# A decoder layer's delta heads: three sums of squares as fp32r products with ones

## The chip, the cores and the metric

The kernel runs on one core of a Trainium2 chip. The metric is the device time of one execution, in microseconds (us). TensorE multiplies (its weight loads are listed as an engine of their own, PEld), VectorE (DVE), ScalarE (ACT) and GpSimd (POOL) work element by element, and SyncE (SP) issues most of the transfers. PSUM is the accumulator that TensorE writes; the kernel uses its eight banks of 128x512 float32 by hand.

## The reference

One hybrid decoder layer over 1024 tokens of width 1024: an RMSNorm, one projection that feeds dilated window attention (12 heads) and a gated DeltaNet (8 heads), sigmoid gates that merge the two, an output projection, and a SwiGLU MLP. What matters here is the DeltaNet branch:

```
qkv = silu(causal_depthwise_conv(concat([qd, kd, vd]), conv_w))
qd = l2norm(qd) * HEAD_DIM_K ** -0.5      # t * rsqrt(sum(t * t) + EPS) over the head's 128
kd = l2norm(kd)
o_d = gated_delta_rule(qd, kd, vd, g, beta)            # chunkwise
o_d = rmsnorm(o_d, dn_norm) * silu(z)                   # o_d * rsqrt(mean(o_d * o_d) + EPS)
```

So each head needs three sums of squares over its 128 channels, of q, of k and of its output, for each of 1024 tokens.

## The kernel before

All is laid out with channels on the 128 partitions and tokens along the free dimension, so a sum over a head's channels is a product with a 128x128 matrix of ones: it sums over partitions and leaves the sum on each of them.

The program is written by hand, engine by engine, with semaphores. `delta_iteration` is one iteration over a delta head. It has 64 steps j. In each step TensorE does one k of the dense projection (`dense_k`, L196: three fp32r products of 128x512, since weights and activations are split into a high and a low part), and beside it stand, in an order fixed by tables, the steps of the recurrence of the head before (`STEPS_AT`: in iteration h they belong to head h-1) and the preparation of head h: the convolution's taps (`TAPS_AT`, DVE), SiLU (`SILU_AT`, ACT), the squares of q and k (`SQUARE_AT`, at j = 47 and 49, ACT), the load of the decay rows (`ROWS_AT`, j = 60, DMAs issued by ACT) and their preparation on DVE (`PREPARE_AT`, j = 62). Every engine runs through its own list of this program in order. Iteration 0 is peeled and has the end of the attention beside it (`attention_end`, whose last mixing on DVE stands at j = 57 and 58, L757 to L764); heads 1 to 7 are a loop (`delta_heads`), and `delta_end` does the last head's recurrence beside the first gate projections, without taps.

The steps on which the change bears:

- `ss` (j = 4): TensorE multiplies ones by `sq[i]` for q and k (L1153, two halves each, float32). ACT takes a logarithm and an exponential of it (L1269, L1272), then DVE makes `qn` and `kn` (L1344, L1347). `kt0` (j = 15, L1167) is the first step of TensorE that waits for `kn`. The merge levels `y1` (L1198) and on follow.
- `a0` to `a7` and `b0` to `b7` (j = 45 to 60): the recurrence over eight chunks of 128 tokens. In `a`, TensorE multiplies by the state (L1247, L1248) and DVE forms `u_now` (L1398). In `b`, TensorE waits for `u_now`, multiplies by it (L1252, L1253), and DVE updates `state` (L1402), for which the next `a` waits.
- in `b3` and `b7`, when four chunks are done, ACT copies half of the output out of PSUM and squares it (L1325, L1326; in the trace `beta_v` and `beta_k`, whose space `o_raw` and `o_sq` share).
- `os` (j = 62): TensorE multiplies ones by `o_sq`, in halves (L1258, float32). `on`, at the end of the iteration, takes logarithm and exponential (ACT, L1330, L1333) and scales the output (DVE, L1406, L1409). Before it ACT reads the dense product `z_next` (L1430, j = 63).

`load_rows` (L1534) issues its three DMAs behind ACT's step b7, and DVE's preparation waits for them at L1458.

Of the kernel before, what the change touches and what calls it, by code (L numbers as in the profile page):

```python
# [65 lines left out]
def build(nc, x, norm_mix, w_in, conv_w, a_log, dt_bias, dn_norm, w_proj_attn, w_proj_delta,  # L66
          w_out, norm_ffn, w_gate, w_up, w_down, norm_final, out):
    ctx = ExitStack()
    with ctx:
# [31 lines left out]
        ident = keep("ident", [P, P])  # L101
        ones = keep("ones", [P, P])
        band = keep("band", [P, 2, 256])
        band_pair = keep("band_pair", [P, P])
# [171 lines left out]
        def setup_pool(pool, then):  # L276
# [23 lines left out]
            for h in range(NHA):  # L300
                g.memset(slopes[:, h:h + 1], float(2.0 ** (-8.0 * (h + 1) / NHA)) * DILATION[h // NSLOT])
            pool.drain().then_inc(consts, 1)

# [763 lines left out]
        def dt_(name, shape):  # L1067
# [25 lines left out]
        a_right, inv_right = dt_("a_right", [P, HALF]), dt_("inv_right", [P, HALF])  # L1093
        assert d0[0] <= work + 81920, d0[0] - work
        u_bar, w_t = inv, half_way
        o_raw, o_sq = beta_v, beta_k

        dl = {x_: sem("dl_" + x_) for x_ in (
            "read", "conv", "silu", "sq", "ss", "ln", "normed", "vt", "bv", "kt", "kdec", "kk", "qk", "rows",
            "diff", "dec", "a", "pt", "t0t", "t0", "t0c", "y", "yc", "ar", "ir", "pr", "prc", "dt", "dtm", "tt", "ttc", "ub", "ubc", "wt", "wtc",  # L1100
            "qdec", "ws", "u", "o", "s", "sup", "z", "os", "osq", "oss", "oln", "oexp", "out", "stored", "zero", "col", "eye")}

# [33 lines left out]
        SILU_AT = {30: 0, 46: 1, 59: 2}  # L1136
        SQUARE_AT = {47: 0, 49: 1}
        ROWS_AT, PREPARE_AT = 60, 62

# [4 lines left out]
        def delta_pe(pe, h, step):  # L1144
            mm, tr = nc.tensor.matmul, nc.tensor.transpose
            two = h * 2
            if step == "ss":
                wait(pe, dl["sup"], h * NCH)
                wait(pe, dl["osq"], two)
                for i in range(2):  # L1150
                    pe.wait_ge(dl["sq"], two + (i + 1))
                    for half in range(2):
                        last = mm(bank[(X0, Y0)[i] + half][:, :], ones[:, :], sq[i][:, half * HALF:(half + 1) * HALF],  # L1153
                                  start=True, stop=True)
                    last.then_inc(dl["ss"], 1)
# [93 lines left out]
            elif step[0] == "b":  # L1249
                c = int(step[1])  # L1250
                pe.wait_ge(dl["u"], h * NCH + (c + 1))
                mm(bank[X1][:, 0:P], chunk(k_dec, c), u_now[:, :], start=True, stop=True).then_inc(dl["s"], 1)  # L1252
                mm(bank[Y0 + c // 4][:, (c % 4) * P:(c % 4 + 1) * P], u_now[:, :], chunk(decay, c),  # L1253
                   start=False, stop=True).then_inc(dl["o"], 1)
            elif step == "os":
                for half in range(2):
                    pe.wait_ge(dl["osq"], two + (half + 1))
                    mm(bank[Z0 + half][:, :], ones[:, :], o_sq[:, half * HALF:(half + 1) * HALF],  # L1258
                       start=True, stop=True).then_inc(dl["oss"], 1)

        def delta_act(act, h, step):
# [59 lines left out]
            elif step in ("b3", "b7"):  # L1321
# [3 lines left out]
                f(o_raw[:, half * HALF:(half + 1) * HALF], bank[Y0 + half][:, :], ACT.Copy)  # L1325
                f(o_sq[:, half * HALF:(half + 1) * HALF], bank[Y0 + half][:, :], ACT.Square).then_inc(dl["osq"], 1)  # L1326
            elif step == "on":
# [7 lines left out]
        def delta_vec(dve, h, step):  # L1335
# [63 lines left out]
            elif step[0] == "b":  # L1399
                c = int(step[1])  # L1400
                dve.wait_ge(dl["s"], h * NCH + (c + 1))
                v.scalar_tensor_tensor(state[:, :], state[:, :], decay_all[:, c:c + 1], bank[X1][:, 0:P],  # L1402
                                       ALU.mult, ALU.add).then_inc(dl["sup"], 1)
            elif step == "on":
                dve.wait_ge(dl["oexp"], h + 1)
                v.scalar_tensor_tensor(o_raw[:, :], o_raw[:, :], dn_norm_c[:, 0:1], o_sq[:, :], ALU.mult, ALU.mult)  # L1406
                dve.drain()
                dve.wait_ge(dl["z"], h + 1)
                v.tensor_tensor(z_now[:, :], o_raw[:, :], z_now[:, :], ALU.mult).then_inc(dl["out"], 1)  # L1409
# [36 lines left out]
        def square_delta_act(act, h, i):  # L1446

            act.wait_ge(dl["silu"], h * 3 + (i + 1))
            wait(act, dl["normed"], h * 2)
            nc.scalar.activation(sq[i][:, :], qkv[i][:, :], ACT.Square).then_inc(dl["sq"], 1)  # L1450

# [41 lines left out]
        def delta_iteration(eng, h, dense, own, side, mix=None):  # L1493

            conv, silu, square, rows_, prepare = own
            for j in range(64):
# [11 lines left out]
                if j in SQUARE_AT:  # L1508
                    square(eng, h, SQUARE_AT[j])
                if j == ROWS_AT:  # L1510
                    rows_(eng, h)
# [24 lines left out]

        OWN_ACT = (nothing, silu_delta_act, square_delta_act, load_rows, nothing)
        OWN_VEC = (conv_vec, nothing, nothing, nothing, prepare_vec)

# [656 lines left out]
        def _(pe):  # L2196
            setup_pe(pe)
            attention(pe, dense_att_pe, att_pe, nothing, decay_pe)
            delta_iteration(pe, 0, dense_delta_pe, [nothing] * 5, att_pe, nothing)

# [3 lines left out]
            pe.wait_ge(o_taken, 6 * NSLOT)  # L2204
            delta_heads(pe, dense_delta_pe, [nothing] * 5, delta_pe)
            delta_end(pe, gate_step_pe, delta_pe)
# [65 lines left out]
```

## Time and profile before

| | |
|---|---|
| three runs | 2349.39 us median, 2349.14 to 2349.42 |
| the profiled execution | 2351.21 us |
| its span in the trace | 2349.5 us |
| mean granted clock of TensorE | 0.987 |
| busy: TensorE (PE), weight loads, DVE, ACT, POOL | 97%, 80%, 41%, 35%, 21% |
| share of the ending chain on TensorE | 91% |
| delta heads' recurrences in the trace | 599.6 to about 1264 us |

A row of a timeline has the start from the span's start and the duration in us, the engine, the line of kernel.py, the operation, output<-inputs with their shapes, and the count of instructions that were merged into the row. In square brackets stands how long the engine was idle before it, and what released it. Durations of matmuls on TensorE overlap, so their pace is read from the starts. A granted clock of 1.00 is 2.4 GHz and 0.50 is 1.2 GHz.

### The profile page before, as it was taken

To read this page: it belongs to the slowest core of one execution; us is meant where nothing else is said; L and a number is where in the kernel's file an instruction comes from. 1 tells how busy PE (TensorE), PEld (TensorE's weight loads), DVE (VectorE), ACT (ScalarE), POOL (GpSimd) and SP (SyncE) were. 2 spreads that over 40 slices of the span, in tenths; PEclk is the share of its full clock that TensorE was granted. 3 is DMA by queue.
4 is the path that set the end of the run, shared out by engine and by line. 5 is a ranking of instruction groups with operands and counts; after the bars stand their busy time and mean duration, and the time that the engine had idled before them with its cause. 6 is when DMAs were issued, how large, how long until landed. Compare 5 with 4: busy or idle time off the path is not lost.

```text
span 2349.5 us, 31341 instructions
## 1 busy us (share of the span) xinstructions
PE 2268.2 (97%) x11304; PEld 1882.0 (80%) x11304; DVE 953.2 (41%) x1360; ACT 811.0 (35%) x1398; POOL 501.2 (21%) x359
## 2 busy tenths in 40 slices
PE   5999999999999999999999999997799999999997
PEld 4788888888788788888878888886688888888886
DVE  3512122122755564565542113332755555550143
ACT  4322323233554555555452220022433333330012
POOL 6253222212211111111112233331000000043330
PEclk8999999999999999999999999999899999999998
DMA  5112121202220221121033443341122222261211
GB/s 119 47 37 64 52 66 45 72 27 44 86 61 17 71 62 36 45 62 62 18 90 101 141 138 117 102 117 45 33 91 83 88 81 80 80 221 47 90 54 72
DMA packets 245975, 174.26 MB, mean 74 GB/s; under 512 B 41160, under 2 KB 223624, under 8 KB 245920
## 3 DMA queue, kind: packets, MB, share of 16 engines
q1 hardware_dynamic: 215856, 129.12, 18.9%
q10 hardware_dynamic: 30064, 44.39, 5.9%
q8 instruction: 36, 0.59, 0.1%
q14 instruction: 19, 0.16, 0.0%
HBM read 142.83 MB, written 30.65 MB: 74 GB/s over the span
## 4 chain that ended last, share of the span: by engine, by line
PE 91%; DVE 4%; ACT 2%; DVEq 1%; issue 1%; POOL 1%; DMA 1%; ACTq 1%; SPq 0%; POOLq 0%
PE bank L196 39%; PE bank L1802 17%; PE bank L2030 10%; PE bank L982 6%; PE bank L1215 2%; PE bank L1198 2%; PE bank L605 1%; PE bank L1153 1%; PE bank L1205 1%; PE bank L616 1%; PE bank L1252 1%; PE bank L1247 1%; PE bank L1248 1%; PE bank L1253 1%; PE bank L1234 1%
## 5 line engine op out<-in xcount | busy, mean ns | idle before, releaser
L196 PE MATMUL bank<-u_hi,w_hi 128*128 128x512 f32 x1472 | 631.0, 429 | 3.0 <-POOL w_lo L184 1.0
L196 PE MATMUL bank<-u_hi,w_lo 128*128 128x512 f32 x1472 | 577.5, 392 | 0.0
L196 PE MATMUL bank<-u_lo,w_hi 128*128 128x512 f32 x1472 | 575.5, 391 | 0.0
L182 POOL CAST w_hi<-raw 128x1024 fp32r<-128x1024 f32 (+1 forms) x108 | 109.5, 1014 | 1152.9 <-PE bank L196 923.9
L196 PEld LDWEIGHTS bank<-u_hi,w_lo 128*128 128x128 f32 x1472 | 276.5, 188 | 60.8
L196 PEld LDWEIGHTS bank<-u_hi,w_hi 128*128 128x128 f32 x1472 | 278.4, 189 | 48.5 <-issue 5.6
L196 PEld LDWEIGHTS bank<-u_lo,w_hi 128*128 128x128 f32 x1472 | 278.9, 189 | 42.3 <-issue 3.8
L184 POOL TENSOR_TENSOR w_lo<-raw,w_hi 128x1024 fp32r<-128x1024 f32 (+1 forms) x108 | 262.3, 2429 | 15.9 <-issue 0.7
L1990 POOL CAST dn_hi<-dn_raw 128x896 fp32r<-128x896 f32 (+1 forms) x24 | 25.4, 1060 | 590.0 <-DMA dn_raw<-in_w_down 481.7
L2030 PE MATMUL bank<-v_lo,dn_hi 128*128 128x512 f32 x352 | 136.9, 389 | 0.0
L2030 PE MATMUL bank<-v_hi,dn_hi 128*128 128x512 f32 x352 | 136.9, 389 | 0.0
L2030 PE MATMUL bank<-v_hi,dn_lo 128*128 128x512 f32 x352 | 136.9, 389 | 0.0
L1489 DVE SCALAR_TENSOR_TENSOR conv_out<-conv_in,conv_c,conv_out 128x1024 f32<-128x1024 f32 (+1 forms) x96 | 100.5, 1047 | 14.9 <-issue 12.0
L1802 PE MATMUL bank<-t_hi_t,p_hi_s 128*128 128x512 f32 x264 | 103.0, 390 | 2.5 <-ACT gate_out L1825 2.5
L1802 PE MATMUL bank<-t_lo_t,p_hi_s 128*128 128x512 f32 x264 | 102.7, 389 | 0.0
L1802 PE MATMUL bank<-t_hi_t,p_lo_s 128*128 128x512 f32 x264 | 102.7, 389 | 0.0
L1378 DVE COPY_PREDICATED inv<-merge_mask,bank 128x256 f32<-128x256 uint8 x96 | 45.5, 491 | 108.6 <-PE bank L1215 108.2
L663 ACT ACTIVATE prob<-score,neg_max 128x256 f32<-128x256 f32 (+1 forms) x96 | 44.6, 465 | 98.9 <-DVE neg_max L725 93.4
L2030 PEld LDWEIGHTS bank<-v_hi,dn_lo 128*128 128x128 f32 x352 | 66.1, 188 | 13.8
L2030 PEld LDWEIGHTS bank<-v_lo,dn_hi 128*128 128x128 f32 x352 | 66.1, 188 | 13.8
L1829 ACT ACTIVATE gate_out<-gate_out 128x512 f32<-128x512 f32 x44 | 27.8, 632 | 142.5 <-DVE gate_out L1845 142.5
L2030 PEld LDWEIGHTS bank<-v_hi,dn_hi 128*128 128x128 f32 x352 | 66.1, 188 | 13.6
(302 smaller groups left out, 3889.1 us busy)
## 6 DMA issues: line engine op xcount, KB each, us to landing
raw<-in_w_in SPq DMA_DIRECT2D x84, 512.0 KB, 3.8
row<-scr_rows ACTq DMA_DIRECT2D x24, 512.0 KB, 4.8
raw_gate<-in_w_gate SPq DMA_DIRECT2D x22, 512.0 KB, 3.8
raw_up<-in_w_up SPq DMA_DIRECT2D x22, 512.0 KB, 3.9
scr_v<-gate_out SPq DMA_DIRECT2D x44, 256.0 KB, 2.5
v_in<-scr_v SPq DMA_DIRECT2D x11, 1024.0 KB, 8.1
scr_gate<-tmp ACTq DMA_DIRECT2D x16, 512.0 KB, 2.9
tmp<-scr_gate ACTq DMA_DIRECT2D x16, 512.0 KB, 4.2
```

Source lines behind the costliest of these rows:

```text
L182: nc.gpsimd.tensor_copy(hi[:, 0:kt, :], raw[slot][:, 0:kt, :])
L184: nc.gpsimd.tensor_tensor(lo[:, 0:kt, :], raw[slot][:, 0:kt, :], hi[:, 0:kt, :].bitcast(F32), ALU.subtract).then_inc(weights_split, 1)
L196: last = nc.tensor.matmul(bank[dst][:, :], wpart[slot][wp][:, k, :], rhs[ap][:, k, half * HALF:(half + 1) * HALF], start=k == 0 and (wp, a ...
L663: last = nc.scalar.activation(prob[p % 2][:, i * w:(i + 1) * w], score[p % 2][:, i * w:(i + 1) * w], ACT.Exp, bias=neg_max[:, b:b + 1], ac ...
L982: last = nc.tensor.matmul(bank[dst][:, :], wpart[slot][wp][:, k, :], branch[ap][:, b, half * HALF:(half + 1) * HALF], start=start and (wp, ...
L1198: last = mm(by_block(chunk(bank[Y0], q), level), chunk(a_right, q), side_columns(inv[:, 2 * q * P:2 * (q + 1) * P], level, 0), start=True, ...
L1215: last = mm(bank[Z0 + half][:, (q % 2) * P:(q % 2 + 1) * P], chunk(inv_t, q), half_pair[:, q, :], start=True, stop=True)
L1378: v.copy_predicated(left(c4(inv, half), level), left(merge_mask[:, level:level + 1, :].broadcast_to([P, 4, P]), level), bank[Z0 + half][:, ...
L1489: last = v.scalar_tensor_tensor(conv_out[:, part], shifted, tap, conv_out[:, part], ALU.mult, ALU.add)
L1802: last = nc.tensor.matmul(dst[:, :], (p_hi, p_lo)[wp][name][:, kk, :], (t_hi, t_lo)[ap][o][:, kk, :], start=i in (0, 1, 3) and kk == 0 and ...
L1829: f(t[:, :], t[:, :], ACT.Silu).then_inc(up["silu"], 1)
L2030: last = nc.tensor.matmul(bank[DN_BANKS[g % 2][i][half]][:, :], dn_part[(n + i) % 4][wp][:, k, :], (v_hi, v_lo)[ap][(k0 + k) // 2][:, (k0 ...
```

## The change

The three products with float32 ones become products of fp32r ones with a high and a low part of the squares, both added up in the same bank. The high part is a cast of the square to fp32r, the low part is square minus high part.

For q and k, ACT squares as before at j = 47 and 49, then drains and casts to `sq_hi`; DVE subtracts at the new steps j = 58 and 60 (`square_low_vec`) and signals `sqlow`, for which TensorE waits in `ss`. `sq_hi` lies where `qn` and `kn` are, so ACT waits for steps that read them (`qdec`, `wt`) instead of `normed`. For the output, ACT drains and casts behind the square in b3 and b7, and signals `osq` only then; DVE waits for `osq` at the end of its own steps b3 and b7, subtracts and signals `osqlow`; TensorE takes high and low part in `os`. A copy of `ones` to `ones_r` is made on POOL in the setup.

```diff
+            g.tensor_copy(ones_r[:, :], ones[:, :])
...
+        sq_hi = [at(f"sq_hi{i}", [P, S], F32R, t) for i, t in enumerate((work + 20480, work + 32768))]
+        o_hi = at("o_hi", [P, S], F32R, work + 53248)
+        o_lo = at("o_lo", [P, S], F32R, work + 65536)
+        sq_lo = [at(f"sq_lo{i}", [P, S], F32R, work + 24576 + 4096 * i) for i in range(2)]
...
         SQUARE_AT = {47: 0, 49: 1}
+        SQUARE_LOW_AT = {58: 0, 60: 1}
...
                 for i in range(2):
-                    pe.wait_ge(dl["sq"], two + (i + 1))
+                    pe.wait_ge(dl["sqlow"], two + (i + 1))
                     for half in range(2):
-                        last = mm(bank[(X0, Y0)[i] + half][:, :], ones[:, :], sq[i][:, half * HALF:(half + 1) * HALF],
-                                  start=True, stop=True)
+                        for part in (sq_hi, sq_lo):
+                            last = mm(bank[(X0, Y0)[i] + half][:, :], ones_r[:, :],
+                                      part[i][:, half * HALF:(half + 1) * HALF],
+                                      start=part is sq_hi, stop=part is sq_lo)
                     last.then_inc(dl["ss"], 1)
...
             elif step == "os":
                 for half in range(2):
+                    hs = slice(half * HALF, (half + 1) * HALF)
                     pe.wait_ge(dl["osq"], two + (half + 1))
-                    mm(bank[Z0 + half][:, :], ones[:, :], o_sq[:, half * HALF:(half + 1) * HALF],
-                       start=True, stop=True).then_inc(dl["oss"], 1)
+                    mm(bank[Z0 + half][:, :], ones_r[:, :], o_hi[:, hs], start=True, stop=False)
+                    pe.wait_ge(dl["osqlow"], two + (half + 1))
+                    mm(bank[Z0 + half][:, :], ones_r[:, :], o_lo[:, hs], start=False, stop=True).then_inc(dl["oss"], 1)
...
-                f(o_sq[:, half * HALF:(half + 1) * HALF], bank[Y0 + half][:, :], ACT.Square).then_inc(dl["osq"], 1)
+                f(o_sq[:, half * HALF:(half + 1) * HALF], bank[Y0 + half][:, :], ACT.Square)
+                act.drain()
+                f(o_hi[:, half * HALF:(half + 1) * HALF], o_sq[:, half * HALF:(half + 1) * HALF],
+                  ACT.Copy).then_inc(dl["osq"], 1)
...
                 v.scalar_tensor_tensor(state[:, :], state[:, :], decay_all[:, c:c + 1], bank[X1][:, 0:P],
                                        ALU.mult, ALU.add).then_inc(dl["sup"], 1)
+                if c % 4 == 3:
+                    hs = slice((c // 4) * HALF, (c // 4 + 1) * HALF)
+                    dve.wait_ge(dl["osq"], two + (c // 4 + 1))
+                    v.tensor_tensor(o_lo[:, hs], o_sq[:, hs], o_hi[:, hs].bitcast(F32), ALU.subtract).then_inc(dl["osqlow"], 1)
...
             act.wait_ge(dl["silu"], h * 3 + (i + 1))
-            wait(act, dl["normed"], h * 2)
-            nc.scalar.activation(sq[i][:, :], qkv[i][:, :], ACT.Square).then_inc(dl["sq"], 1)
+            wait(act, dl["qdec"], h)
+            wait(act, dl["wt"], h * 2)
+            nc.scalar.activation(sq[i][:, :], qkv[i][:, :], ACT.Square)
+            act.drain()
+            nc.scalar.activation(sq_hi[i][:, :], sq[i][:, :], ACT.Copy).then_inc(dl["sq"], 1)
+
+        def square_low_vec(dve, h, i):
+
+            dve.wait_ge(dl["sq"], h * 2 + (i + 1))
+            nc.vector.tensor_tensor(sq_lo[i][:, :], sq[i][:, :], sq_hi[i][:, :].bitcast(F32),
+                                    ALU.subtract).then_inc(dl["sqlow"], 1)
...
                 if j in SQUARE_AT:
                     square(eng, h, SQUARE_AT[j])
+                if j in SQUARE_LOW_AT:
+                    square_low(eng, h, SQUARE_LOW_AT[j])
```

## Rows read from the trace of the kernel before

**Rows 1.** The page: busy time and share of TensorE; chain that ended last, by engine.

```profile
PE 2268.2 (97%) x11304; PEld 1882.0 (80%) x11304; DVE 953.2 (41%) x1360; ACT 811.0 (35%) x1398; POOL 501.2 (21%) x359
...
PE 91%; DVE 4%; ACT 2%; DVEq 1%; issue 1%; POOL 1%; DMA 1%; ACTq 1%; SPq 0%; POOLq 0%
```

**Rows 2.** Groups by line: shapes, xcount | busy us, mean ns | idle before.

```profile
L1153 PE MATMUL bank<-sq,ones 128*128 128x512 f32 x64 | 28.8, 592 | 0.0
...
L1258 PE MATMUL bank<-beta_k,ones 128*128 128x512 f32 x32 | 15.0, 592 | 0.0
```

**Rows 3.** Timeline, step ss of head 0: start us, us, engine, instruction.

```profile
599.85 3.60 PE L1153 MATMUL bank<-sq,ones 128*128 128x512 f32 x8
...
603.52 0.39 PE L196 MATMUL bank<-u_lo,w_hi 128*128 128x512 f32 x1
```

**Rows 4.** Chain that ended last, output projection: start us, us of 24 dense matmuls.

```profile
1559.79 5.46 PE bank L196 x24
```

**Rows 5.** Timeline, end of b7 and step os of head 0.

```profile
680.21 0.59 ACT L1326 ACTIVATE beta_k<-bank 128x512 f32<-128x512 f32 x1
...
680.90 1.88 PE L1258 MATMUL bank<-beta_k,ones 128*128 128x512 f32 x4
```

**Rows 6.** Timeline, steps b3 to b4 of head 0.

```profile
670.38 0.35 DVE L1402 SCALAR_TENSOR_TENSOR state<-state,decay_all,bank 128x128 f32<-128x128 f32 x1
...
670.60 0.60 ACT L1325 ACTIVATE beta_v<-bank 128x512 f32<-128x512 f32 x1 [2.77 <-PE bank L1253]
...
670.83 0.75 DVE L1489 SCALAR_TENSOR_TENSOR conv_out<-conv_in,conv_c,conv_out 128x512 f32<-128x512 f32 x1
...
671.09 0.59 ACT L1326 ACTIVATE beta_k<-bank 128x512 f32<-128x512 f32 x1
...
671.51 0.29 DVE L1398 TENSOR_TENSOR u_now<-inv,bank 128x128 f32<-128x128 f32 x1
...
672.23 0.38 PE L1252 MATMUL bank<-u_now,k_dec 128*128 128x128 f32 x2
```

**Rows 7.** Groups by line of other stages: casts on ACT, a subtraction on DVE.

```profile
L1714 ACT ACTIVATE p_hi_s<-p_sum_s 128x512 fp32r<-128x512 f32 x88 | 52.7, 622 | 8.2 <-DVE p_sum_s L1724 6.1
...
L948 ACT ACTIVATE b_hi<-tmp 128x1024 f32 x12 | 12.6, 1054 | 0.9 <-DMA tmp<-scr_branch 0.9
...
L1729 DVE TENSOR_TENSOR p_lo_s<-p_sum_s,p_hi_s 128x512 fp32r<-128x512 f32 x88 | 56.5, 684 | 0.0
```

**Rows 8.** Timeline of DVE, the preparation behind head 1's row DMAs.

```profile
687.39 0.17 DVE L1458 COPY decay_all<-row 128x8 f32<-128x8 f32 x1 [7.44 <-DMA row<-scr_rows]
```

**Rows 9.** Timeline of head 1, from the normalisation of q and k to kt0.

```profile
694.75 1.23 DVE L1344 SCALAR_TENSOR_TENSOR qn<-qkv,sq 128x1024 f32<-128x1024 f32 x1 [0.80 <-ACT sq L1272]
...
695.89 1.22 DVE L1347 TENSOR_TENSOR kn<-qkv,sq 128x1024 f32<-128x1024 f32 x1
...
698.59 0.60 PE L1167 MATMUL bank<-ident,kn 128*128 128x128 f32 x4
```

**Rows 10.** Timeline around head 0's sums, beside the end of the attention.

```profile
603.74 1.23 DVE L764 TENSOR_TENSOR joint<-joint,o_t 128x1024 f32<-128x1024 f32 x1
...
606.05 0.50 PE L196 MATMUL bank<-u_hi,w_hi 128*128 128x512 f32 x1 [0.55 <-ACT z_next L1430]
...
615.07 0.66 PE L1167 MATMUL bank<-ident,kn 128*128 128x128 f32 x4 [2.38 <-DVE kn L1347]
```

**Rows 11.** Timeline, step y1 of head 0 and of head 1.

```profile
625.67 1.07 PE L1198 MATMUL bank<-inv,a_right 128*128 128x128 f32 x8
...
708.79 1.07 PE L1198 MATMUL bank<-inv,a_right 128*128 128x128 f32 x8
```

**Rows 12.** Timeline; then stretches: us, busy by engine (x), granted clock, DMA share, GB/s.

```profile
47.29 0.79 PE L406 MATMUL bank<-u_hi,w_ba_hi 128*128 128x512 f32 x1 [3.68 <-POOL u_lo L307]
...
47.20:50.00 2.80, 2.71 (x6) 2.15 (x7) 0.00 (x0) 0.00 (x0) 2.65 (x3) 0.52 0.00 0
...
615.00:618.00 3.00, 2.93 (x21) 2.72 (x22) 3.00 (x2) 2.65 (x7) 2.26 (x1) 1.00 0.00 0
```

More of the change, by code:

```diff
@@ L102, in build @@
         ones = keep("ones", [P, P])
+        ones_r = keep("ones_r", [P, P], F32R)
         band = keep("band", [P, 2, 256])
@@ L1098, in build @@
         dl = {x_: sem("dl_" + x_) for x_ in (
-            "read", "conv", "silu", "sq", "ss", "ln", "normed", "vt", "bv", "kt", "kdec", "kk", "qk", "rows",
+            "read", "conv", "silu", "sq", "sqlow", "ss", "ln", "normed", "vt", "bv", "kt", "kdec", "kk", "qk", "rows",
             "diff", "dec", "a", "pt", "t0t", "t0", "t0c", "y", "yc", "ar", "ir", "pr", "prc", "dt", "dtm", "tt", "ttc", "ub", "ubc", "wt", "wtc",
-            "qdec", "ws", "u", "o", "s", "sup", "z", "os", "osq", "oss", "oln", "oexp", "out", "stored", "zero", "col", "eye")}
+            "qdec", "ws", "u", "o", "s", "sup", "z", "os", "osq", "osqlow", "oss", "oln", "oexp", "out", "stored", "zero", "col", "eye")}
         def side_columns(t, level, side):
@@ L1493, in delta_iteration @@
         def delta_iteration(eng, h, dense, own, side, mix=None):
-            conv, silu, square, rows_, prepare = own
+            conv, silu, square, square_low, rows_, prepare = own
             for j in range(64):
@@ L1534, in load_rows @@
                 act.dma_start(row[j][:, :], src.rearrange("a t -> (a t)").partition_broadcast(P)).then_inc(dl["rows"], 16)
-        OWN_ACT = (nothing, silu_delta_act, square_delta_act, load_rows, nothing)
-        OWN_VEC = (conv_vec, nothing, nothing, nothing, prepare_vec)
+        OWN_ACT = (nothing, silu_delta_act, square_delta_act, nothing, load_rows, nothing)
+        OWN_VEC = (conv_vec, nothing, nothing, square_low_vec, nothing, prepare_vec)
         def store_delta(sp, h):
@@ L2198, in _ @@
             attention(pe, dense_att_pe, att_pe, nothing, decay_pe)
-            delta_iteration(pe, 0, dense_delta_pe, [nothing] * 5, att_pe, nothing)
+            delta_iteration(pe, 0, dense_delta_pe, [nothing] * 6, att_pe, nothing)
             pe.wait_ge(st_copied, 3 * NSLOT)
@@ L2204, in _ @@
             pe.wait_ge(o_taken, 6 * NSLOT)
-            delta_heads(pe, dense_delta_pe, [nothing] * 5, delta_pe)
+            delta_heads(pe, dense_delta_pe, [nothing] * 6, delta_pe)
             delta_end(pe, gate_step_pe, delta_pe)
```

## The prediction

> **What bounds the kernel now.** I read the page first: TensorE is busy for 97% of the span and the chain that ended last lies 91% on it [rows 1]. A saving counts only where TensorE keeps its pace, and every wait put into its way costs in full. Then the groups by line: the ones products stand in the trace as 64 and 32 records, two to one 128x512 product, so 32 products for q and k and 16 for the output [rows 2]. Last the timelines of one head, with one question: when does each input of a changed step arrive, and when does TensorE come for it? The figures below are of head 0, whose steps begin at 599.85 us, and from its end at 680.9 us on of head 1; the next heads repeat them to a few hundredths of a us, save where I say so.
>
> **The products.** From the first ones record of q and k to the second dense matmul behind them pass 603.52 - 599.85 = 3.67 us [rows 3]. A dense fp32r matmul takes 5.46 / 24 = 0.227 us [rows 4], so the four float32 products take 3.67 - 0.23 = 3.44 us, 0.86 us each. After the change they are eight fp32r ones, 8 x 0.227 = 1.82 us: 1.62 us less in a head. The two of the output, from 680.90 on [rows 5], take 1.72 us by the same measure and become four, 0.91 us: 0.81 us less. With every input in time that is 8 x 2.43 = 19.4 us. Now the inputs.
>
> **q and k, heads 1 to 7: 1.3 us gained each.** Squares, casts and low parts are ready before TensorE comes: ACT has 2.77 us free ahead of its b3 step [rows 6] and gets two casts there (1054 ns for 128x1024 [rows 7]), 2.1 us; the two low parts (like kn's 1.22 us for the same shape [rows 9]) lie on DVE at j=58 and 60, where its taps are over, and ahead of its 7.44 us wait for the row DMA [rows 8]. Behind the sums ACT's two logarithms and exponentials go on from z_next at j=63 and do not move; kn is ready at 695.89 + 1.22 = 697.11, TensorE comes for it at 698.59 [rows 9]. It will come at 696.97, so it waits 0.2 us, plus 0.1 us for a weight load that is no longer hidden (a dense matmul right behind a wait lasts 0.50 us [rows 10], one in the stream 0.39 [rows 3]). Net 1.62 - 0.3 = 1.3 us; seven heads, -9.2 us. With no wait it is -11.3, with the row DMAs 1 us later reaching kn (DVE has 0.80 us of slack ahead of qn [rows 9]) some -8.
>
> **The output's step os: nothing gained.** The second half is squared by ACT until 680.21 + 0.59 = 680.80 [rows 5]. Behind it stand a drain and a cast (622 ns for 128x512, [rows 7]), to 681.5, then DVE's subtraction (684 ns, [rows 7]), to 682.2. The last product starts at 682.25, loads its weights in the open, and ends near 682.6, where the float32 version ends today (680.90 + 1.72 = 682.6). 0 us; the bounds over eight heads are -6.5 (all hidden) and +4 (each of the two operations slower by a quarter of a us).
>
> **Step b3, the new wait: 2.1 us lost per head.** At c = 3 DVE now waits for osq and subtracts before it goes on. DVE works its list in order, so behind the wait stand the conv tap of j=52 and u_now of chunk 4, for which TensorE's step b4 waits. ACT's square ends at 671.09 + 0.59 = 671.68 [rows 6]; drain and cast to 672.35; low part to 673.1; the tap starts 0.1 us later (as today behind state, 670.73 to 670.83) at 673.2, and u_now 0.68 us after the tap's start (671.51 - 670.83), at 673.9 instead of 671.51: 2.4 us late [rows 6]. u_now ends today at 671.80 and b4 starts at 672.23, which leaves 0.4 us of slack. TensorE loses 2.0 us, and 0.1 us for the open weight load: 2.1 us. Afterwards DVE needs about 2.1 us a chunk (two taps of 0.68, a state of 0.35, a u_now of 0.29, and the gaps between them), and TensorE takes twice 671.51 - 670.38, 2.26 us; so DVE catches up in two chunks without a further stall. Seven heads, +14.7 us; bounds 1.8 and 2.5 each (+12.6, +17.5). The last head has the same timing but no taps, so u_now would start at 673.05 in place of 671.51: 1.5 us late, less 0.4, plus 0.1: +1.2 us.
>
> The Trainium skill, "TensorE: Matmul & The Clock Gate", section "Architectural detail", says that ScalarE and VectorE take their queues strictly in order, and only TensorE pulls weight loads ahead. By that rule this wait is paid in full; were it not so, the sum would be without its largest term, about 16 us lower.
>
> **The normalisation of head 0: 3.2 us lost.** Here DVE has no idle time in front: the mixing of the attention output runs until 603.74 + 1.23 = 604.97 [rows 10], and the low part of q comes behind it in DVE's list, that of k behind that. They are ready at 606.1 and 607.3, but TensorE comes for them at 599.85 [rows 3]. It stands for 6.3 us, finishes both sums at 608.3, and after nine dense matmuls is at 610.4 where today it is at 606.05 [rows 10]: 4.3 us behind. Today it then waits until 615.07 for kn (2.38 us [rows 10]); it will come at 616.7 with kn ready at about 615. From there I take the flow of head 1, 10.2 us from kt0 at 698.59 to the first merge level at 708.79, which brings that level to 626.9 instead of 625.67 [rows 9, 11]: 1.3 us lost. On top comes the clock. After a gap of 3.68 us the granted clock was 0.52 over the next 2.8 us, after the 2.38 us gap at kn it was 1.00 [rows 12]. So after 6.3 us TensorE starts at 1.2 GHz; eight matmuls at 0.43 instead of 0.23 us cost 1.6 to 1.9 us, which nothing hides, since it is late already. Together +3.2 us, bounds +0.5 and +5.
>
> The same page, section "What's actually happening", says that an idle array falls back to half rate and is released again by sustained work; by it the 1.9 us are due, without it the first head costs 1.3 us.
>
> **Small parts, taken as nothing.** The copy into ones_r is one 128x128 operation on POOL in the setup, where POOL then waits for the first activations. The waits for qdec and wt at j=47 ask for steps of j=19 and 43. The row DMAs are issued about 1 us later, behind drain and cast; DVE waits for them anyway [rows 8], and what follows has that 0.8 us of slack [rows 9]. With this cover gone it would be 0.2 us a head.
>
> **Sum.** -9.2 + 0 + 14.7 + 1.2 + 3.2 = +9.9 us. The profiled execution took 2351.21 us with a span of 2349.5; the median of the runs is 2349.39, so I add the difference to the median, **2359.3 us**, or 2361.1 for a profiled execution.
>
> **The rivals.**
> 1. The wait at b3 does not reach TensorE (u_now is not held up, or osq arrives early enough). For it: each part is off TensorE, and DVE has time left in this stage. Against: the times of rows 6, which put ACT's square alone past u_now. The rest stays: -9.2 + 3.2 = -6.0, **2343.4 us**, faster. It decides for this side as soon as the stall at b3 falls below about 0.3 us a head; with the first head free too it is 2340. Chance 0.08.
> 2. The stalls exist but are smaller: b3 at 1.7 us (the tap runs closer behind), no slow clock and no loss in the first head: -9.2 + 11.9 + 1 = +3.7, **2353 us**, no change. Chance 0.14.
> 3. DVE does not catch up: the chunks behind b4 lose another 0.3 us, and os 0.5 us, in each of eight heads: +6.4 on the sum, **2365.7 us**. For it: DVE's load of 2.1 in 2.28 us leaves little. Against: state is due 0.4 us after DVE can have it. Chance 0.18.
> 4. The forecast, 0.60.
> That an fp32r product with ones is no faster is excluded by rows 2 to 4, shape for shape.
>
> **Numbers.** Slower by over 0.2% (4.7 us, about what a measurement of this kernel tells from no change) are the forecast, rival 3 and a little of rival 2: 0.80. Within: 0.12. Faster: 0.08. The range reaches from within rival 2 to rival 3's centre, 2352 to 2366, and leaves out rival 1 and the upper tail.
>
> **What the profile after will show.** The group of L1153 becomes two forms of fp32r, 0.227 us apart, 64 products, the output's 32. At b4 TensorE and its weight load stand idle for about 2 us on DVE's u_now in seven heads and 1.1 us in the last. At kt0 it waits about 0.2 us on kn. In the first head it stands for some 6 us before the first sum, followed by a granted clock near 0.5, and no longer waits at kn. The period of a head grows by about 0.8 us. The prediction is wrong if u_now of chunk 4 starts less than 1 us later than today relative to b3, or if the period falls.

## The result, and the profile of the changed kernel

The changed kernel takes 2370.35 us (2368.80 to 2372.88), the kernel before 2349.40 us (2349.14 to 2353.06) beside it: the ratio is 1.0086, 95% interval 1.0073 to 1.0099. It is slower, as forecast, but by 20.9 us where 9.9 were forecast, and above the range of 2352 to 2366. The profiled execution took 2370.46 us with a span of 2368.7. One of the four executions of the output-only kernel below took 2878.87 us at a mean granted clock of 0.749, a slower state of the chip, and is left out of its numbers.

Start with the places that the prediction named. The timeline of b3 and b4 in head 0 of the changed kernel (start us, us, engine, instruction) shows the chain that it worked out, link by link:

```profile
671.20 0.60 ACT L1336 ACTIVATE beta_v<-bank 128x512 f32<-128x512 f32 x1 [0.51 <-PE bank L1262]
...
671.70 0.59 ACT L1337 ACTIVATE beta_k<-bank 128x512 f32<-128x512 f32 x1
...
672.36 0.63 ACT L1339 ACTIVATE o_hi<-beta_k 128x512 fp32r<-128x512 f32 x1
...
673.02 0.69 DVE L1421 TENSOR_TENSOR o_lo<-beta_k,o_hi 128x512 fp32r<-128x512 f32 x1 [1.69 <-ACT o_hi L1339]
673.82 0.75 DVE L1516 SCALAR_TENSOR_TENSOR conv_out<-conv_in,conv_c,conv_out 128x512 f32<-128x512 f32 x1
674.48 0.28 DVE L1412 TENSOR_TENSOR u_now<-inv,bank 128x128 f32<-128x128 f32 x1
...
674.82 0.49 PE L1261 MATMUL bank<-u_now,k_dec 128*128 128x128 f32 x2 [1.81 <-DVE u_now L1412]
```

From ACT's copy at the end of b3 to u_now of chunk 4 pass 674.48 - 671.20 = 3.28 us, where they were 671.51 - 670.60 = 0.91 us [rows 6]: 2.37 us late, 2.4 forecast. The waits of TensorE over the seven loop heads and the last one (engine, line waited for: us in total, times, longest):

```profile
PE bank L1261 <- DVE u_now L1412: 13.7, 8, 1.8
PE bank L1270 <- DVE o_lo L1421: 1.9, 8, 0.2
PE bank L1224 <- issue: 1.3, 7, 0.2
PE bank L1176 <- DVE kn L1361: 1.0, 3, 0.5
```

In the kernel before, the same list held only the third line. A wait list tells what an engine stood for, not how fast it ran afterwards. That is in the granted clock. The stretches right behind the stall in head 0 (us, TensorE's busy time (x), granted clock, DMA share, GB/s):

```profile
673.20:674.80 1.60, 0.00 (x0) 1.00 0.00 0
674.90:676.10 1.20, 1.20 (x8) 1.00 0.00 0
676.10:679.60 3.50, 3.50 (x14) 0.54 0.01 2
679.60:684.00 4.40, 4.40 (x28) 0.98 0.00 0
```

TensorE resumes at 674.82 at 2.4 GHz, and some 1.6 us later, inside the third of these stretches, its clock falls to 1.2 GHz for 3.4 us. The matmuls show it too, a dense one lasting 0.63 us instead of 0.39:

```profile
675.60 0.39 PE L197 MATMUL bank<-u_lo,w_hi 128*128 128x512 f32 x1
...
677.17 0.63 PE L197 MATMUL bank<-u_lo,w_hi 128*128 128x512 f32 x1
```

This happens in all seven loop heads, and not in the last head, whose stall is 0.96 us. Four stretches of 10 us, from 2 us behind the copy of b3, in heads 0, 2, 6 and the last:

```profile
673.20:683.20 10.00, 8.38 (x42) 0.83 0.00 1
844.52:854.52 10.00, 8.38 (x42) 0.83 0.00 0
1186.39:1196.39 10.00, 8.38 (x42) 0.83 0.00 0
1272.49:1282.49 10.00, 9.24 (x54) 1.00 0.00 0
```

This is the reading by which the experiments below are judged: 0.83 means that the clock fell in that head, 1.00 that it did not.

**Where the 19.2 us of span went.** ACT's copy at the end of b3 and the one at the end of b7 cut each head in two. The sums of the pieces in the two profiled executions:

| stretch | before | after | difference | forecast |
|---|---|---|---|---|
| b3 to b7, seven loop heads | 7 x 9.12 | 7 x 12.8 | +25.9 | +14.7 |
| b3 to b7, last head | 9.12 | 10.35 | +1.2 | +1.2 |
| b7 to the next b3, seven times | 517.3 | 509.6 | -7.7 | -9.2 |
| span's start to the first b3 | 670.6 | 671.2 | +0.6 | +3.2 |
| last b7 to the end | 1088.7 | 1087.9 | -0.8 | 0 |

One line is off by more than 3 us, and it is the one with the slow clock in it.

### The profile page after: what moved, and what is told of

Its sections match the earlier page's. It is cut to its first block, busy times and chain, and to the rows that moved or that the text cites. A ratio compares the mean times of both kernels' runs of the same rounds, so it can differ in the third digit from the quotient of the medians.

```text
span 2368.7 us, 31452 instructions
## 1 busy us (share of the span) xinstructions
PE 2267.4 (96%) x11304; PEld 1887.4 (80%) x11304; DVE 985.9 (42%) x1392; ACT 838.2 (35%) x1430; POOL 504.2 (21%) x360
## 4 chain that ended last, share of the span: by engine, by line
PE 87%; DVE 4%; ACT 2%; DMA 2%; DVEq 1%; issue 1%; ACTq 1%; POOL 1%; SPq 0%; POOLq 0%
PE bank L197 37%; PE bank L1831 17%; PE bank L2059 10%; PE bank L984 6%; PE bank L1224 2%; PE bank L1207 2%; DMA row<-scr_rows 1%; PE bank L607 1%; PE bank L1214 1%; PE bank L1261 1%; PE bank L618 1%; PE bank L1262 1%; PE bank L1243 1%; PE bank L1181 1%; PE bank L1237 1%
## 5 line engine op out<-in xcount | busy, mean ns | idle before, releaser
L185 POOL TENSOR_TENSOR w_lo<-raw,w_hi 128x1024 fp32r<-128x1024 f32 (+1 forms) x108 | 263.9, 2444 | 15.6 <-issue 0.2
L1516 DVE SCALAR_TENSOR_TENSOR conv_out<-conv_in,conv_c,conv_out 128x1024 f32<-128x1024 f32 (+1 forms) x96 | 100.6, 1048 | 16.0 <-issue 13.7
L2059 PEld LDWEIGHTS bank<-v_hi,dn_hi 128*128 128x128 f32 x352 | 66.1, 188 | 14.2 <-POOL dn_lo L2021 0.4
```

The costliest lines, as they stand in the source:

```text
L185: nc.gpsimd.tensor_tensor(lo[:, 0:kt, :], raw[slot][:, 0:kt, :], hi[:, 0:kt, :].bitcast(F32), ALU.subtract).then_inc(weights_split, 1)
L1516: last = v.scalar_tensor_tensor(conv_out[:, part], shifted, tap, conv_out[:, part], ALU.mult, ALU.add)
L2059: last = nc.tensor.matmul(bank[DN_BANKS[g % 2][i][half]][:, :], dn_part[(n + i) % 4][wp][:, k, :], (v_hi, v_lo)[ap][(k0 + k) // 2][:, (k0 ...
```

## The experiments

**Theory.** The stall at b4 is as forecast, and it brings the clock down behind it; that second cost is what was missed. **Rival.** The missing 11 us have another cause (the new products, VectorE's backlog, a clock that falls in this stage anyway), and the slow clock is no consequence of the stall.

All kernels were timed beside the kernel before, which gave 2350.55 to 2351.06 us in these sessions. The full table first; "b3 to b7" in us, "slow heads" are loop heads in which the clock fell, both read from one profiled execution of each kernel:

| kernel | median us | wait at b4 | b3 to b7 | slow heads |
|---|---|---|---|---|
| before | 2350.9 | none | 9.12 | 0 of 7 |
| changed | 2370.35 | 1.81 | 12.8 | 7 of 7 |
| changed, again | 2370.25 | 1.81 | 11.34 / 12.8 | 6 of 7 |
| q and k only | 2344.72 | none | 9.12 | 0 of 7 |
| output only | 2367.70 | 1.81 | 11.27 / 12.8 | 2 of 7 |
| low part at chunk 6 | 2346.97 | none | 9.12 | 0 of 7 |
| filled, 8 products | 2363.67 | about 0.1 | 11.35 | 0 of 7 |
| filled, 4 products | 2363.06 | 0.9 | 11.34 | 0 of 7 |
| shifted by 0.45 us | 2370.00 | 1.81 | 11.34 / 12.8 | 4 of 7 |
| shifted by 1.36 us | 2370.13 | 1.81 | 11.34 / 12.8 | 2 of 7 |
| longer stall | 2388.71 | 3.42 | 12.88 / 14.2 to 15.6 | 6 of 7 |
| os at j=63 | 2343.52 | none | 9.12 | 0 of 7 |
| and head 0 early | 2342.93 | none | 9.12 | 0 of 7 |
| and kn first | 2344.23 | none | 9.12 | 0 of 7 |

The setup, ahead of this stage, varies from execution to execution (the first b3 lay between 669.4 and 674.3 us), so medians of two kernels closer than some 2 us are not told apart, and the intervals inside the traces are what the verdicts rest on.

**1. The q and k part alone.** The output goes back to one float32 product per half, and with it ACT's second cast and VectorE's wait go.

```
-                if c % 4 == 3:
-                    hs = slice((c // 4) * HALF, (c // 4 + 1) * HALF)
-                    dve.wait_ge(dl["osq"], two + (c // 4 + 1))
-                    v.tensor_tensor(o_lo[:, hs], o_sq[:, hs], o_hi[:, hs].bitcast(F32), ALU.subtract).then_inc(dl["osqlow"], 1)
...
+                    mm(bank[Z0 + half][:, :], ones[:, :], o_sq[:, half * HALF:(half + 1) * HALF],
+                       start=True, stop=True).then_inc(dl["oss"], 1)
```

> Only the q and k part of the change; the output's sum of squares stays the float32 product of the kernel before. My theory (the 2.0 us stall at b4 and the slow clock that follows it are the whole of what the prediction missed): no wait at b4, b3 to b7 back to 9.1 us, the granted clock after it 1.00 in all heads; what is left is -1.2 to -1.3 us in each of seven heads and +3.0 in head 0's normalisation, so 2349.4 - 8.7 + 3.0 = 2343.7 us. The rival (the missing 11 us have another cause, in the q and k part or in the clock of the stage as a whole): 2350 to 2355 us, with a lower clock somewhere in heads 1 to 7 although nothing stalls.

Measured: 2344.72 us (2342.83 to 2345.69), ratio 0.9971 (0.9960 to 0.9982), 6.1 us below the kernel before. b3 to b7 is 9.12 us in all heads. b7 to the next b3 is 72.6 us instead of 73.94 in six of the seven intervals, which is the 1.3 us per head of the prediction; the seventh, beside the first gate projection, is 73.30 instead of 73.56, since TensorE stands there for ACT to take that projection out of its bank (`tmp`). No wait on u_now, o_lo or kn is left among TensorE's:

```profile
PE bank L1224 <- issue: 1.3, 7, 0.2
PE bank L197 <- ACT tmp L916: 0.9, 1, 0.9
```

So the cast and low-part work for q and k is harmless; everything unforeseen comes with the output's part.

**2. The output part alone.** The products for q and k are float32 again, with no casts and low parts for them.

> Only the output part of the change; q and k are summed in float32 as before. My theory: seven heads lose 2.07 us of stall and 1.65 us of slow clock each, 26.0, and the last head 1.2, so 2349.4 + 27.2 = 2376.6 us, with b3 to b7 at 12.8 us. The rival, by which the stall alone belongs to this part: 2349.4 + 14.5 + 1.2 = 2365 us, with b3 to b7 at 11.2 us and no slow clock.

Measured: 2367.70 us (2366.69 to 2370.94, three executions), ratio 1.0067 (1.0047 to 1.0087). The 16.8 us lost lie near the rival's 15.7, and the profiled execution, the slowest of the three, lies between the two numbers. Its trace says why. The stall is the same in all heads (8 waits, 13.7 us in sum), but the clock fell in two of the seven only. Heads 0, 1 and 4:

```profile
671.74:681.74 10.00, 8.39 (x42) 0.83 0.00 1
758.51:768.51 10.00, 8.39 (x50) 1.00 0.00 0
1014.21:1024.21 10.00, 8.38 (x42) 0.83 0.00 0
```

b3 to b7 takes 11.27 us where it held and 12.8 where it fell. That splits the 3.7 us of the changed kernel: 2.15 us for the stall (2.1 forecast; 2.2 in the heads of the kernels with the whole change in which the clock held) and 1.5 us for the slow clock. The sum 5 x 2.15 + 2 x 3.7 + 1.2 = 19.4 us agrees with this execution, whose span is 2369.2 - 2349.5 = 19.7 us above that of the kernel before. The run also damaged the theory in its first form, "the stall brings the clock down": the same stall does so in one head and not in the next.

**3. The wait moved, nothing else.**

```
                 v.tensor_tensor(u_now[:, :], chunk(u_bar, c), bank[X0][:, 0:P], ALU.subtract).then_inc(dl["u"], 1)
+                if c == 6:
+                    dve.wait_ge(dl["osq"], two + 1)
+                    v.tensor_tensor(o_lo[:, 0:HALF], o_sq[:, 0:HALF], o_hi[:, 0:HALF].bitcast(F32),
+                                    ALU.subtract).then_inc(dl["osqlow"], 1)
...
-                if c % 4 == 3:
+                if c == 7:
```

> The whole change, but the low part of the output's first half is taken by VectorE behind u_now of chunk 6 instead of behind the state of chunk 3; nothing else moves. My theory: no stall at b4 and no fall of the clock, b3 to b7 at 9.1 us as before, 7 x 3.7 + 1.2 = 27 us back: 2343 us, which is below the kernel before. The rival (the clock falls in this stage anyway, because the recurrence gives TensorE little to do): only the stall comes back, 15.7 us, 2354.7 us, with a clock near 0.55 for 3.5 us in each head.

Measured: 2346.97 us (2343.98 to 2348.28), ratio 0.9982 (0.9972 to 0.9991). b3 to b7 is 9.12 us in every head and the clock 1.00; 23 us came back with the whole of the computation in place. The rival, by which the recurrence slows down anyway, falls here. The 4 us above the expected 2343 lie outside b3 to b7: the profiled execution entered its first b3 at 673.4 us instead of 671.2, and some of the stretches from b7 to b3 were up to 0.4 us longer than the 72.6 of run 1, with waits for kn of up to 0.4 us.

**4. The stall filled.** Eight fp32r products of 128x512 that nothing reads, on TensorE ahead of its wait at b4; u_now is as late as before.

```
+                if c == 4 and not isinstance(h, int):
+                    for _ in range(8):
+                        mm(bank[Z0][:, :], ones_r[:, :], act_in[0][:, 0, 0:HALF], start=True, stop=True)
                 pe.wait_ge(dl["u"], h * NCH + (c + 1))
```

> The whole change, with VectorE's wait left where it is, and in the seven loop heads eight more fp32r products of 128x512 on TensorE ahead of its wait at b4, 8 x 0.227 = 1.8 us of work whose results nothing reads. u_now comes as late as before, so the time lost by lateness stays. My theory (idle time of TensorE is what brings the clock down): TensorE waits 0.3 us or less at b4, the clock stays at 1.00, and 7 x 1.65 = 11.5 us come back: 2359 us, about the predicted time. The rival (lateness costs 3.7 us a head by itself, or the slow clock has another cause): 2370 us or more, with the clock near 0.55 behind b4 as in the changed kernel.

Measured: 2363.67 us (2363.15 to 2364.30), where 2359 were expected. The clock held in all heads and b3 to b7 went from 12.8 to 11.35 us (11.6 in head 0). Over the seven heads that is 10.1 us; the median fell by 6.7. In the trace the rest lies outside: the first b3 came 1.1 us later, and from the last b7 to the end passed 2.0 us more. Adding work made the kernel faster, which leaves the idleness of TensorE as what brings the slow clock and excludes the lateness of u_now. Head 1, a stretch like those above:

```profile
758.52:768.52 10.00, 10.00 (x58) 1.00 0.00 0
```

**5. Half filled.** The same with `range(4)`.

> The whole change with four in place of eight unread fp32r products ahead of the wait at b4 in the seven loop heads: the stall is cut from 2.1 to about 1.1 us, u_now comes as late as ever. If the length of the stall decides (0.96 us left the clock alone in the last head): clock 1.00, b3 to b7 11.3 us, 2363 us. If any stall at this place brings the clock down: b3 to b7 12.8 us, 2370 us.

Measured: 2363.06 us (2361.87 to 2364.99), 2363 expected. The wait at b4 is 0.9 us, and the clock holds in 7 of 7 heads. The waits of the eight heads, then the stretch in head 1:

```profile
PE bank L1264 <- DVE u_now L1415: 7.2, 8, 1.0
```

```profile
757.59:767.59 10.00, 9.11 (x54) 1.00 0.00 0
```

The last heads of six other traces, whose wait is 0.95 or 0.96 us, show no fall either, and none lies behind the waits for kn of up to 1.2 us in run 10 and 1.4 us in run 12.

**6 and 7. The stall as it is, at another moment.** Runs 1 to 5 leave open why 7 heads fell in one kernel and 2 in another. The stall returns once a head, every 85.4 to 85.7 us in the changed kernel. Unread products ahead of b0 change nothing at b4 but move the next stall: six of them first (1.36 us), then two (0.45 us).

```
+                if c == 0 and not isinstance(h, int):
+                    for _ in range(6):
+                        mm(bank[Z0][:, :], ones_r[:, :], act_in[0][:, 0, 0:HALF], start=True, stop=True)
```

> The whole change with its full stall at b4, and six unread fp32r products, 1.36 us of busy TensorE, ahead of b0 in the seven loop heads: the stall is the same, only its moment moves by another 1.36 us from head to head. They cost 7 x 1.36 = 9.5 us themselves. If the stall alone decides: slow clock in 7 of 7 heads, b3 to b7 12.8 us in each, 2370.4 + 9.5 = 2380 us. If it also depends on the moment at which the stall falls, as the run of the output part alone suggests (2 of 7 heads slow at the same stall): some heads at 11.3, some at 12.8, and 1.5 us less for each at 11.3, 2371 to 2378 us.

> The whole change with its full stall and two unread fp32r products (0.45 us) ahead of b0 in the seven loop heads, a third of the shift that left 2 of 7 heads slow. They cost 3.2 us themselves. If the moment of the stall matters and drifts from head to head: fewer than 7 heads with b3 to b7 at 12.8 us, the others at 11.3, about 2 to 5 slow ones, 2366 to 2371 us. If the changed kernel's 7 of 7 is a property of the stall and the larger shift did something else: 7 of 7 again, 2373.5 us.

Measured: 2370.13 us (2368.03 to 2375.37) with six, 2 of 7 heads slow; 2370.00 us (2368.11 to 2371.45) with two, 4 of 7 slow. The six products are 9.5 us of work in seven heads; in the trace the intervals from b7 to b3 are 8.5 us longer, and the five heads whose clock held gave 7.4 us back. The wait is 1.81 us in each of these heads; heads 4 and 5 of the first, then 0 and 1 of the second:

```profile
1019.67:1029.67 10.00, 8.38 (x50) 1.00 0.00 0
1105.30:1115.30 10.00, 8.38 (x42) 0.83 0.00 0
```

```profile
671.89:681.89 10.00, 8.38 (x42) 0.83 0.00 1
757.88:767.88 10.00, 8.39 (x50) 1.00 0.00 0
```

The same kernel, the same stall, the same work around it, one head slow and the next not: what differs is when the stall comes. The granted clock of the changed kernel shows it as a drift. Two neighbouring stretches in head 0, whose stall ended at 674.82, and two in head 6, whose stall ended at 1188.01:

```profile
676.10:676.40 0.30, 0.30 (x4) 0.97 0.00 0
676.40:676.70 0.30, 0.30 (x4) 0.50 0.00 0
...
1188.10:1188.40 0.30, 0.30 (x3) 0.97 0.00 0
1188.40:1188.70 0.30, 0.30 (x4) 0.50 0.00 0
```

Read in stretches of 0.1 us, the fall comes 1.56, 1.23, 0.91, 0.79, 0.60, 0.46 and 0.37 us behind the end of the stall in heads 0 to 6. The stalls are 85.4 to 85.7 us apart, the falls 85.33 or 85.34 us, all six times. So the clock falls at moments that keep a time of their own and are not tied to the stall. The Trainium skill, "TensorE: Matmul & The Clock Gate", section "What's actually happening", says that the gate watches TensorE's activity by a raster of its own that runs on freely and does not start with the kernel. These runs agree, with falls at equal distances behind stalls at unequal ones, and with 2, 4, 6 and 7 of 7 heads at one and the same 1.81 us wait.

This also answers whether the filled kernels of runs 4 and 5 were only lucky in their moments. Their loop heads are 84.0 to 84.5 us apart, so against the falls' 85.33 us the moment moves by about 1 us from head to head, and none of the fourteen fell.

**8. A longer stall.** VectorE holds u_now of chunk 4 back by two more operations that leave the values as they are, with a drain ahead of each and one more ahead of the signal `osqlow`.

```
+                    if c == 3:
+                        for _ in range(2):
+                            dve.drain()
+                            v.tensor_tensor(o_lo[:, hs], o_lo[:, hs].bitcast(F32), o_lo[:, hs].bitcast(F32), ALU.max)
```

> The whole change, and VectorE holds u_now of chunk 4 back by two more operations of 0.68 us (each takes the maximum of the low part with itself, the values stay), so the stall at b4 grows from 2.1 to about 3.5 us; that of the last head from 1.0 to 2.4 us. The moment from head to head moves too, by 1.4 us. If the length of the stall makes the fall of the clock more likely (1.1 us: 0 of 7, 2.1 us: 2 of 7 or 7 of 7 by its moment): slow in all seven, b3 to b7 14.2 us or more, 2370.4 + 9.8 = 2380 us. If at any length above some 2 us the moment alone decides: 2 to 4 of 7 heads slow, the others at 12.7 us, 2373 to 2376 us.

Measured: 2388.71 us (2387.06 to 2388.74), above both expectations, whose sums left out the last head. The wait is 3.42 us, the clock fell in 6 of 7 loop heads and now also in the last, whose wait went from 0.96 to 2.70 us. Head 1, the one that held, head 2, and the last:

```profile
761.89:771.89 10.00, 6.78 (x41) 1.00 0.00 0
847.52:857.52 10.00, 6.77 (x33) 0.83 0.00 0
1285.17:1295.17 10.00, 7.49 (x36) 0.83 0.00 0
```

From b3 to b7 the seven heads take 100.3 us instead of 89.7 and the last 13.69 instead of 10.35, 14 us more in all. The other 4 us of the 18.4 were not in the heads' b3 to b7 stretches; 1.6 of them lie ahead of the first b3 and 2.2 behind the last b7. Even 3.4 us is not a sure fall, since one head held. And a fall need not wait for TensorE to resume: in heads 3, 5 and 6 it came 0.3, 0.8 and 0.4 us before the end of the stall. In head 5 the clock then stayed low for 6.8 us instead of 3.4, and b3 to b7 took 15.6 us, 2.7 more than in the head that held. Its stall ended at 1112.48:

```profile
1111.60:1112.40 0.80, 0.00 (x0) 0.55 0.00 0
1112.50:1118.50 6.00, 6.00 (x20) 0.50 0.00 0
```

**9. The changed kernel again.**

> The changed kernel once more, nothing altered: does a second execution show the slow clock in 7 of 7 heads again? If the number goes by the kernel's own period (its stall comes every 85.5 us): 6 or 7 of 7 again, 2370 us. If it goes by when the stage happens to begin: another number, and a time lower by 1.5 us for each head less, 2362 to 2370 us.

Measured: 2370.25 us (2367.69 to 2372.48), 6 of 7 slow. Head 5 held, head 6 did not:

```profile
1103.36:1113.36 10.00, 8.38 (x50) 1.00 0.00 0
1187.42:1197.42 10.00, 8.38 (x41) 0.83 0.00 0
```

Two traces with 7 and 6 slow heads, against 2 and 4 in runs 6 and 7: the high count comes back with the kernel. But it is not a matter of the period alone. In run 6 heads 1 to 4 held, 85.3 to 85.6 us apart, about as far as the slow heads of the changed kernel. In the five traces with the 1.81 us wait, the next head did as the one before in 18 of 21 intervals of 85.2 to 85.8 us, near the 85.33 us of the falls, and in 1 of 9 others (84.1 to 84.4 and 86.0 to 87.1 us). So a period of about 85.4 us repeats whatever the head before did, and the changed kernel has it when its clock falls. These counts were made after the runs, and no run was built to test them, so this stays a reading.

**10 to 12. Is the rest of the output part worth having?** These three build on run 3. In that run os still had its gap: `o_lo` of the second half 0.23 us late, two weight loads in the open. Moved from j=62 to j=63:

```
-                    62: ["os"], 63: ["on"]}
+                    63: ["os", "on"]}
```

> The kernel with the low part behind u_now of chunk 6, and in addition the output's sums (step os) one dense step later, at j=63 in place of j=62. In the kernel without this move TensorE stood 0.23 us for o_hi's and o_lo's second half in the middle of os and loaded two weights in the open: first product to next dense matmul 1.71 us where four products take 0.91. My theory: with three dense matmuls (0.68 us) more in front the inputs are ready and 0.7 us come back in each of eight heads, 2347.0 - 5.6 = 2341.4 us. The rival (os hides behind nothing: ScalarE's logarithms for the output then come later and hold up the next head): 2347 us or more.

Measured: 2343.52 us (2340.96 to 2345.62), ratio 0.9970 (0.9957 to 0.9982). The four products now stand 0.24 us apart:

```profile
684.51 0.40 PE L1268 MATMUL bank<-o_hi,ones_r 128*128 128x512 f32 x1
684.75 0.40 PE L1270 MATMUL bank<-o_lo,ones_r 128*128 128x512 f32 x1
684.98 0.40 PE L1268 MATMUL bank<-o_hi,ones_r 128*128 128x512 f32 x1
685.22 0.48 PE L1270 MATMUL bank<-o_lo,ones_r 128*128 128x512 f32 x1
```

Yet from b7 to the next b3 the mean of six heads is 72.65 us, against 72.75 without the move. The list of waits shows where the gain went; first without the move, then with it:

```profile
PE bank L1270 <- DVE o_lo L1425: 1.6, 7, 0.2
...
PE bank L1176 <- DVE kn L1361: 0.9, 3, 0.4
```

```profile
PE bank L1176 <- DVE kn L1361: 3.7, 5, 1.2
```

TensorE arrives earlier at kt0 and stands there for kn. The median is 3.4 us below that of run 3, but 3.0 us of the difference between the two traces lie behind the last b7. Next, k was normalised ahead of q on VectorE, since kt0 needs k alone:

```
+                dve.wait_ge(dl["ln"], two + 2)
+                v.tensor_tensor(kn[:, :], qkv[1][:, :], sq[1][:, :], ALU.mult).then_inc(dl["normed"], 1)
                 v.scalar_tensor_tensor(qn[:, :], qkv[0][:, :], float(P) ** -0.5, sq[0][:, :], ALU.mult,
                                        ALU.mult).then_inc(dl["normed"], 1)
```

> As the run with os at j=63, and VectorE normalises k before q (the next step of TensorE needs k only); the waits for q move to the step that reads it. In the run without this edit kt0 waited for kn in five of seven heads, 3.7 us together, up to 1.2 us, behind qn's 1.22 us. My theory (the gain of os went into this wait): the wait at kt0 is gone, b7 to the next b3 falls from 72.7 to about 72.0 us in each of seven heads, 4 to 5 us in all: 2339 us. The rival (what is late is the rows' transfer, and the next step in line, vt or kk, waits instead): 2343 us as before.

Measured: 2344.23 us (2340.53 to 2345.54), mean 72.63 us. The wait for kn is gone and another took its place, VectorE's inv_t at step t0 (j=19); from TensorE's waits of this kernel:

```profile
PE bank L1195 <- DVE inv_t L1379: 1.6, 3, 0.8
```

The rival of that run was right in kind: in all seven heads VectorE begins this work when the rows' transfer has landed (`decay_all` waits 1.0 to 2.2 us for it, as in [rows 8]), and what is gained ahead of it is lost at the first step behind it. And head 0, with VectorE's low parts ahead of the mixing:

```
+                low_at = SQUARE_LOW_AT if mix is None else {55: 0, 56: 1}
```

> As the run with os at j=63, and in head 0 alone VectorE takes the two low parts of q and k at j=55 and 56, ahead of the mixing of the attention output, instead of behind it. My theory (head 0 loses its 3 us because TensorE stands 6 us for low parts that wait behind the mixing): no stall at the first sum, no slow clock behind it, a wait of some 2.5 us for kn as in the kernel before, 3 us less than without this edit: 2338.5 us. The rival (the mixing, now 2.4 us later, sets ScalarE's z_next and with it the normalisation): the 2.4 us come back at kn and the time stays within 1 us of the run without the edit.

Measured: 2342.93 us (2342.44 to 2346.22), ratio 0.9970 (0.9959 to 0.9982). The first sums come without a wait, as expected, and the wait is back nine matmuls later:

```profile
601.88 0.39 PE L197 MATMUL bank<-u_hi,w_lo 128*128 128x512 f32 x1
607.05 0.80 PE L197 MATMUL bank<-u_hi,w_hi 128*128 128x512 f32 x1 [4.78 <-ACT z_next L1452]
```

The mixing ends 2.4 us later, ACT's z_next stands behind it in ACT's queue, and TensorE's bank waits for z_next; the clock is low here too, in this trace from 605.1 us, inside the wait of 4.78 us, until 611.9. The rival was right: no gain that a measurement shows.

So the best versions end between 2342.9 and 2344.7 us, 6 to 8 us below the kernel before, and the q and k part alone is one of them. The output's half of the change brings nothing measurable here even when its wait costs nothing.

## Why the prediction was wrong

**What held.** The chain at b3, link by link (u_now 2.37 us late, 2.4 forecast); the stall's own price, 2.15 us against 2.1, read where the clock held; the last head, +1.2 and +1.2; q and k in six of seven intervals, -7.5 us against -7.9 (the seventh, beside the gate projection, gained 0.3 instead of 1.3 us: TensorE stood 0.5 us for kn and 0.3 us for ACT's `tmp`, a wait that the prediction did not have), so -7.7 against -9.2 in all; nothing gained at os; VectorE caught up without further stall, so rival 3 did not come, though its 2365.7 us is nearer to the result than the forecast. Head 0's first sums waited 6.14 us (6.3 forecast), and the clock was at 1.2 GHz when they began:

```profile
603.80 0.80 PE L1161 MATMUL bank<-sq_hi,ones_r 128*128 128x512 f32 x1 [6.14 <-DVE sq_lo L1476]
```

From the moment at which TensorE came for them, 603.80 - 6.14 = 597.66, to the first b3 pass 73.5 us, where it was 670.60 - 599.85 = 70.8: +2.8 against +3.2. The table above has only +0.6 for it because this execution entered the stage 2.2 us earlier. The working behind this term is looser than its result: by its own rows TensorE comes for kn at 615.07 - 2.38 + 4.3 = 617.0, not 616.7, and no row shows its eight slow matmuls; the clock fell at 601.3, inside the wait, and stayed low until 608.1, 4.3 us behind the first sum's start.

**What failed** is one term: "TensorE loses 2.0 us, and 0.1 us for the open weight load: 2.1 us" at b3, seven times. It priced the stall by its length alone and put the clock behind it at nothing without giving a reason, although the same text, one section on, charged the clock for the 6.3 us stall of head 0. The term measured 25.9 us against 14.7; 7 x 1.5 = 10.5 of the 11.2 us between them are the slow clock, as the output part alone, the filled stalls and the shifted ones separate it. Without it the result would have been near 2360 us. That this is so close to the forecast of 2359.3 is partly luck: q and k gained 1.5 us less than forecast, and a start 2.6 us earlier than forecast and an end 0.8 us shorter hide that in the profiled execution.

**Why it was left out.** The prediction does not say why the clock stands nowhere in its term for b3. The trace before held two idle stretches beside a granted clock [rows 12]: 3.68 us with 0.52 behind it, 2.38 us with 1.00. A 2.0 us stall is shorter than the one that did no harm, which makes it look harmless. Runs 2, 6, 7 and 9 show what that row was worth: one case, of a thing that goes one way or the other. The same 1.81 us wait was harmless in 14 heads and not in 21 (of 35 loop heads in five profiled executions), and one of seven waits of 3.42 us was harmless. The right term would have been 1.5 us times a share of the heads between none and all, 0 to +10.5 us on the sum; the range should have reached to 2370 at least. None of the rivals had the clock at b3; that is the mechanism that was missing among them.

## What to carry to other kernels

Price a new stall on TensorE in two parts: the time it stands, and the slow stretch that may follow (here 1.5 us behind a 1.8 us wait, when it came, and none behind 0.9 to 1.4 us). If it repeats in a loop, multiply the second part by anything from none to all of the iterations, and let the range hold both ends; one harmless gap in a trace excludes nothing.

When a wait must be added on an engine that also feeds the critical chain, place it where its input is long there: three chunks later the same operation cost nothing, and 23 us came back. And before making a step cheaper look at what it hands over to: what q and k gained arrived, what os gained ended as a wait on work behind a transfer.

## What the runs showed of the hardware

The clock fell at 21 of 35 waits of 1.81 us, at none of those of 0.9 to 1.4 us, and at 6 of 7 of those of 3.42 us. At the 1.81 us waits it fell 0.1 to 1.6 us after work had resumed, never in the wait; at those of 3.42 us it fell between 0.8 us before the end of the wait and 1.5 us behind it. In the changed kernel's trace the falls were 85.33 or 85.34 us apart, the stalls 85.4 to 85.7. One fall put the clock at 1.2 GHz for 3.4 us, once for 6.8 us, and cost about 1.5 us, that once 2.7 us, in a head whose TensorE was otherwise full. Eight products that nobody reads, put into the stall, cost no time of their own and saved that 1.5 us.

A product with ones in two fp32r parts of 128x512 takes 0.23 us a part, 0.47 us together (run 10's four starts are 0.24 us apart), against 0.86 us in float32 [rows 3]. Whether that is worth having hangs on the engine that makes the parts: a cast of 0.63 us on ACT and a subtraction of 0.69 us on VectorE for each 128x512.
